# Seven products instead of eight in the last two column blocks of two output projections

## What is computed

```python
x = x + diff_attention(rms_norm(x, a_norm_g[0]), ...)       # ends in  o @ w_o      (2048 x 2048)
x = x + sq_relu_mlp(rms_norm(x, mlp_norm_g[0]), w_up[0], w_down[0])
k_nope, k_rope, v = shared_latent_kv(x, ...)
x = x + mla_attention(rms_norm(x, b_norm_g[0]), ...)        # ends in  o @ b_w_o    (2048 x 2048)
x = x + sq_relu_mlp(rms_norm(x, mlp_norm_g[1]), w_up[1], w_down[1])
return rms_norm(x, final_norm_g)
```

## Time and profile before

| | us |
|---|---|
| median of 3 runs | 1980.34 (1980.28 to 1980.65) |
| the profiled execution, its own time | 1980.67 |
| its span | 1977.9 |
| PE busy (matmul) | 1968.6 |
| DVE busy | 1649.0 |
| ACT busy | 1221.1 |

### The profile page before, as it was taken

How to read it: one execution, slowest core, us unless ns; L and a number is a source line. 1 busy time by engine, 2 the same in 40 slices (tenths; PEclk the granted TensorE clock), 3 DMA queues, 4 the chain that set the end, 5 groups by cost and what they waited for, 6 DMA issues and landing times.

```text
span 1977.9 us, 24520 instructions
## 1 busy us (share of the span) xinstructions
PE 1968.6 (100%) x9080; PEld 1641.7 (83%) x9080; DVE 1649.0 (83%) x2015; ACT 1221.1 (62%) x1563; POOL 34.4 (2%) x45
## 2 busy tenths in 40 slices
PE   9999999999999999999999999999999999999998
PEld 7888888888888888888888998888888888888887
DVE  7789996678988998898886787667998898898886
ACT  6555555557667566656656665556566666666663
POOL 0000000000000000000000000000000000000000
PEclk9999999999999999999999999999999999999999
DMA  8655546766787587677666554676587678658663
GB/s 306 214 171 188 175 167 204 225 199 216 224 243 232 189 243 234 218 231 225 224 213 213 146 152 143 229 222 223 194 231 234 224 228 241 207 205 256 216 233 118
DMA packets 269405, 418.23 MB, mean 211 GB/s; under 512 B 18800, under 2 KB 88816, under 8 KB 269296
## 3 DMA queue, kind: packets, MB, share of 16 engines
q1 hardware_dynamic: 254096, 396.87, 61.1%
q0 software_dynamic: 3456, 12.58, 3.4%
q10 hardware_dynamic: 11744, 7.34, 1.3%
HBM read 379.00 MB, written 2.10 MB: 193 GB/s over the span
## 4 chain that ended last, share of the span: by engine, by line
PE 97%; issue 2%; DVE 0%; ACT 0%; POOL 0%; POOLq 0%; DVEq 0%; ACTq 0%
PE acc L617 23%; PE acc L619 23%; PE acc L618 23%; PE side L852 3%; PE side L853 3%; PE side L851 3%; PE acc L851 2%; PE acc L853 2%; PE acc L852 2%; PE acc L637 2%; PE acc L638 2%; PE acc L639 2%; PE acc L966 1%; PE acc L967 1%; PE acc L968 1%
## 5 line engine op out<-in xcount | busy, mean ns | idle before, releaser
L1745 DVE TENSOR_TENSOR wlo<-raw,whi 128x1024 fp32r<-128x1024 f32 (+2 forms) x564 | 669.5, 1204 | 141.5 <-ACT whi L1113 139.9
L1113 ACT ACTIVATE whi<-raw 128x1024 fp32r<-128x1024 f32 (+2 forms) x564 | 579.2, 1046 | 331.1 <-PE acc L619 264.3
L617 PE MATMUL acc<-whi,opA 128*128 128x512 f32 (+2 forms) x1072 | 414.7, 387 | 0.0
L619 PE MATMUL acc<-whi,opA 128*128 128x512 f32 (+2 forms) x1072 | 413.9, 386 | 0.0
L618 PE MATMUL acc<-wlo,opA 128*128 128x512 f32 (+2 forms) x1072 | 413.8, 386 | 0.0
L617 PE MATMUL acc<-whi,opB 128*128 128x512 f32 x976 | 381.1, 390 | 0.0
L619 PE MATMUL acc<-whi,opB 128*128 128x512 f32 x976 | 380.0, 389 | 0.0
L618 PE MATMUL acc<-wlo,opB 128*128 128x512 f32 x976 | 379.8, 389 | 0.0
L619 PEld LDWEIGHTS acc<-whi,opA 128*128 128x128 f32 x1072 | 201.3, 188 | 40.2
L617 PEld LDWEIGHTS acc<-whi,opA 128*128 128x128 f32 x1072 | 201.3, 188 | 40.0
L618 PEld LDWEIGHTS acc<-wlo,opA 128*128 128x128 f32 x1072 | 201.3, 188 | 40.0
(11 more groups left out here) (382 smaller groups left out, 2733.9 us busy)
## 6 DMA issues: line engine op xcount, KB each, us to landing
raw<-in_w_up SPq DMA_DIRECT2D x128, 1024.0 KB, 5.9
raw<-in_w_down SPq DMA_DIRECT2D x128, 1024.0 KB, 5.1
raw<-in_a_w_qkv SPq DMA_DIRECT2D x44, 1024.0 KB, 5.1
prob<-o_sb SPq DMA_DIRECT2D x136, 128.0 KB, 2.6
raw<-in_a_w_o SPq DMA_DIRECT2D x16, 1024.0 KB, 5.1
raw<-in_b_w_o SPq DMA_DIRECT2D x16, 1024.0 KB, 5.1
raw<-in_w_ukv SPq DMA_DIRECT2D x32, 256.0 KB, 4.2
xs<-junk POOLq DMA_DIRECT2D x12, 512.0 KB, 5.3
```

The source lines that it names most:

```text
L617: mm(o, a_hi, w_hi, start=start, stop=False)
L619: done = mm(o, a_lo, w_hi, start=False, stop=last and c == chunks - 1)
L1113: done = fn(whi[:, place:place + ch, 0:n], raw[:, r, c0:c0 + ch, 0:n], ACT.Copy)
L1745: done = tt_(wlo[:, place:place + ch, 0:n], raw[:, r, c0:c0 + ch, 0:n], whi[:, place:place + ch, 0:n].bitcast(F32), ALU.subtract)
```

## The change

In each output projection blocks 0 and 1 stay plain, and so do row chunks 0 to 7 and 12 to 15 of blocks 2 and 3. Row chunks 8 to 11 of blocks 2 and 3 together become one group of `seven`. The functions `seven`, `shares_free`, `combine`, `form_sums`, `form_low`, `form_high`, `copy_shared`, `low` and `down_form` are moved out of `mlp` unchanged so that `out_proj` can call them, and the counts by which groups, shares and form sets are numbered take the new group in. What is new:

```diff
@@ SP @@
-            with sp.Fori(0, JB) as j:
-                whole(B_WO + j, W_O, NB * j)
+            def out_proj(b0, w, v0):
+                with sp.Fori(0, 2) as j:
+                    whole(b0 + j, w, NB * j)
+                for i, (j, r) in enumerate(((2, 0), (2, 1), (2, 2), (3, 2), (2, 3), (3, 0), (3, 1), (3, 3))):
+                    quad(b0 + 2 + i // 4, i % 4, w[:, 4 * r:4 * r + 4, NB * j:NB * j + NB], later=int(i == 6))
+                    if i in (1, 4):
+                        move_chunk(v0 + i // 4)
@@ PE @@
-                for j in range(1, JB):
-                    s = (j + 1) % 2
-                    block_tok(b0 + j, s, uses[s] + j // 2, opB)
+                block_tok(b0 + 1, 0, uses[0], opB)
+                b = b0 + 2
+                for hf in range(4):
+                    half_tok(b, hf, 1, chunks_of(opB, 2 * hf), first=hf == 0, uses=uses[1] + 1)
+                shares_free(SHARE["out", l])
+                pe.wait_ge(form_lo, FORM_SETS * l + 1)
+                seven(GROUP["out", l], b, 4, opB, 8, [forms[0][:, i] for i in range(2)], uses[0] + 1, True, SHARED)
+                for hf in range(2):
+                    half_tok(b + 1, hf, 1, chunks_of(opB, 12 + 2 * hf), last=hf == 1)
+                for hf in range(2, 8):
+                    half_tok(b + 1, hf, 0, chunks_of(opB, 2 * hf - 4 if hf < 6 else 2 * hf), first=hf == 2, last=hf == 7,
+                             uses=uses[0] + 1, starts=(False, True))
@@ ACT @@
                 x_squares(v0, 1, uses[1] + 1)
-                for j in range(1, JB):
-                    s = (j + 1) % 2
-                    body(b0 + j, {4: lambda: x_move(v0 + j - 1), 7: lambda: x_hi(v0 + j - 1, gain)})
-                    x_squares(v0 + j, s, uses[s] + j // 2 + 1)
+                body(b0 + 1, {6: lambda: form_high(forms[0][:, 0], FORM_SETS * l),
+                              7: lambda: x_hi(v0, gain)})
+                x_squares(v0 + 1, 0, uses[0] + 1)
+                b = b0 + 2
+                split(b, 3)
+                seven(GROUP["out", l], b, 4, (2, b), (3, b), {"T4": lambda: x_hi(v0 + 1, gain)})
+                for hf in range(4):
+                    split(b + 1, hf)
+                act.wait_ge(xsq, 2 * (v0 + 2))
+                copy_shared()
+                for hf in range(4, 8):
+                    split(b + 1, hf)
+                act.wait_ge(out_added, 2 * l + 2)
+                x_squares(v0 + 2, 1, uses[1] + 2)
+                split(b + 2, 0)
+                x_move(v0 + 2)
+                split(b + 2, 1)
+                split(b + 2, 2)
+                x_hi(v0 + 2, gain)
+                x_squares(v0 + 3, 0, uses[0] + 2)
@@ DVE @@
                 add_product(b0, 1, uses[1], slice(0, NB))
                 x_turn(v0, 1, 2 * (uses[1] + 1))
-                for j in range(1, JB):
-                    s = (j + 1) % 2
-                    body(b0 + j, {7: lambda: x_lo(v0 + j - 1, gain)})
-                    add_product(b0 + j, s, uses[s] + j // 2, slice(NB * j, NB * j + NB))
-                    x_turn(v0 + j, s, 2 * (uses[s] + j // 2 + 1))
+                body(b0 + 1, {4: out_form_sums, 7: lambda: x_lo(v0, gain),
+                              8: lambda: form_low(down_form(0), FORM_SETS * l)})
+                add_product(b0 + 1, 0, uses[0], slice(NB, 2 * NB))
+                x_turn(v0 + 1, 0, 2 * (uses[0] + 1))
+                b = b0 + 2
+                seven(GROUP["out", l], b, 4, (2, b), (3, b), 8 * b + 3,
+                      {"first sum": lambda: split(b, 3), "T4": lambda: x_lo(v0 + 1, gain)})
+                for hf in range(4):
+                    split(b + 1, hf)
+                combine(SHARE["out", l], down_shared)
+                split(b + 1, 4)
+                dve.wait_ge(pe_halves, 8 * b + 10)
+                add_product(None, 1, uses[1] + 1, slice(2 * NB, 3 * NB))
+                split(b + 1, 5)
+                dve.wait_ge(drained[1], 2 * (uses[1] + 2))
+                share_added()
+                split(b + 1, 6)
+                dve.wait_ge(out_added, 2 * l + 2)
+                x_turn(v0 + 2, 1, 2 * (uses[1] + 2))
+                split(b + 1, 7)
+                split(b + 2, 0)
+                split(b + 2, 1)
+                split(b + 2, 2)
+                x_lo(v0 + 2, gain)
+                add_product(b + 1, 0, uses[0] + 1, slice(3 * NB, 4 * NB))
+                x_turn(v0 + 3, 0, 2 * (uses[0] + 2))
```

More of the change, by code:

```diff
@@ new lines, in copy_shared, with seven @@
+            def copy_shared():
+                for k in range(4):
+                    fn(down_shared[k], side[k], ACT.Copy).then_inc(shared_copied, 1)
+            def seven(group, b, hf0, own, other, between):
+                (o, o_loads), (t, t_loads) = own, other
+                source = {"B11": raw[:, o, 0:2, :], "B21": raw[:, o, 2:4, :], "B22": raw[:, t, 2:4, :],
+                          "T1": w_sum, "T2": raw[:, t, 2:4, :], "T3": raw[:, t, 0:2, :], "T4": w_sum}
+                for f in FORMS:
+                    if f in SUMS:
+                        act.wait_ge(w_summed, 4 * group + SUMS[f])
+                    elif f == "B22":
+                        act.wait_ge(raw_ready[t], 16 * t_loads + 16)
+                    else:
+                        act.wait_ge(raw_ready[o], 16 * o_loads + 16)
+                    if f in IN_EXTRA:
+                        e = extra_number(group, f)
+                        if e >= 2:
+                            act.wait_ge(pe_extra, e - 1)
+                        place = 2 * (e % 2)
+                        fn(extra_hi[:, place:place + 2, :], source[f], ACT.Copy).then_inc(extra_hi_ready, 1)
+                    else:
+                        hf = hf0 + IN_RING.index(f)
+                        act.wait_ge(pe_halves, 8 * b + hf - 3)
+                        fn(whi[:, 2 * (hf % 4):2 * (hf % 4) + 2, :], source[f], ACT.Copy).then_inc(hi_ready, 1)
+                    if f in between:
+                        between[f]()
@@ new lines, in seven @@
+            def seven(group, b, hf0, own, other, lows_before, after):
+                (o, o_loads), (t, t_loads) = own, other
+                n, e = 4 * group, 3 * group
+                b11, b21 = raw[:, o, 0:2, :], raw[:, o, 2:4, :]
+                b12, b22 = raw[:, t, 0:2, :], raw[:, t, 2:4, :]
+                dve.wait_ge(raw_ready[o], 16 * o_loads + 16)
+                dve.wait_ge(raw_ready[t], 16 * t_loads + 16)
+                dve.wait_ge(lo_ready, lows_before)
+                tt_(w_sum, b11, b12, ALU.add).then_inc(w_summed, 1)
+                after["first sum"]()
+                dve.wait_ge(w_summed, n + 1)
+                tt_(b12, b12, b22, ALU.add).then_inc(w_summed, 1)
+                if "second sum" in after:
+                    after["second sum"]()
+                low("B22", group, b, hf0, b22)
+                low("T1", group, b, hf0, w_sum)
+                dve.wait_ge(w_summed, n + 2)
+                dve.wait_ge(lo_ready, 8 * b + hf0 + 1)
+                tt_(b22, w_sum, b22, ALU.add).then_inc(w_summed, 1)
+                low("B21", group, b, hf0, b21)
+                dve.wait_ge(w_summed, n + 3)
+                dve.wait_ge(extra_lo_ready, e + 1)
+                tt_(w_sum, b22, b21, ALU.add).then_inc(w_summed, 1)
+                low("B11", group, b, hf0, b11)
+                if "B11" in after:
+                    after["B11"]()
+                low("T2", group, b, hf0, b22)
+                if "T2" in after:
+                    after["T2"]()
+                low("T3", group, b, hf0, b12)
+                dve.wait_ge(w_summed, n + 4)
+                low("T4", group, b, hf0, w_sum)
+                if "T4" in after:
+                    after["T4"]()
```

271 lines of the change are left out of this document (111 added, 160 removed).

## The result

The changed kernel takes **1986.48 us** (median of 10 runs, 1984.90 to 1989.31) against 1980.43 for the kernel before (10 runs, 1979.70 to 1981.27): a ratio of 1.0032, with a 95% interval of 1.0022 to 1.0041. It is slower, by 6.05 us. I had said 1982.9, from 1977.7 to 1986.0, and most likely "no change": the range misses it by 0.5 us, and the likeliest case was the wrong one. The profiled execution is 1985.44 long, against 1980.67 before; their spans are 1983.5 and 1977.9.

What follows compares the result with a forecast made beforehand. PE was taken to bound the kernel: -2.3 us on its list and +4.9 in two waits made +2.6, so 1982.9 us against the median, range 1977.7 to 1986.0.

Steps and rivals of the forecast that it cites:

- no change: Whole kernel: within 0.2% (4.0 us) of before, on the slow side; this outcome was given 63%.
- The landings: Third and fourth chunks' moves, first issue to last landing: 8.0 to 9.6 us, taken as 8.9 for all four.
- what PE saves: PE's list in the output projections: a group's 42 matmuls replace 48 plain ones, saving 1.15 us a layer, 2.3 in both.
- the group does not starve PE: Output projection blocks with the group: DVE's work fits, so no PE wait; the rival that it starves PE had 5%.
- The half microsecond: First half behind the group, layer 0: remainder ready at 356.4, PE wants it at 357.0, so no wait counted.
- my 0.3: DVE between the second and third turn: no gap over 0.3 us expected in the changed profile.
- The two turns: DVE, layer 0: third turn ends some 57 us after block 0's addition begins (before 46.9), fourth some 71.5 (before 68.6).
- the moves again 8.9: Fourth chunk's moves behind its turn at 386.3: 8.9 us, then rounding and remainder 2.2, complete at 397.5; PE waits 2.4.
- the rival of the long landings: Third and fourth chunks' moves as long as their own before, 8.55 to 9.65 us: +4.2, 1984.5 us; chance 30%.
- break-even at 8.25 us: Third and fourth chunks' moves: two landings of 8.25 us are the break-even.
- behind each turn the change keeps their order: SP's weight loads beside ACT's moves: order unchanged behind each turn; sharing engines packet by packet speaks for late landings.
- Moving the first two chunks' moves there I cost at nothing either way: First two chunks' moves put on SP: no cost or gain, since the up projection reads them only two blocks later.

Runs made afterwards that it cites:

- experiment 4: The change, but with the first two chunks' moves issued by ACT again instead of SP: 1987.99 us, ratio 1.0037.
- experiment 5: The change, but with the third chunk's turn behind the last remainder of block 3 instead of ahead of it: 1982.45 us, ratio 1.0008.
- experiment 1: The change, but with the third and fourth chunks' moves issued by SP too, between the loads: 1978.19 us, ratio 0.9989.
- experiment 7: The change, plus 8 and 18 unused matmuls on PE ahead of the fourth and seventh half, where it waits: 1985.54 us, ratio 1.0028.
- experiment 8: The kernel before, all products plain and no group, with all four chunks' moves issued by SP: 1980.17 us, ratio 0.9997.
- experiment 6: The kernel before, without the group, with the third turn late, just ahead of the last remainder of block 3: 1982.93 us, ratio 1.0014.
- 9: The change with only the third chunk's moves put on SP, the fourth's left on ACT: 1978.33 us, ratio 0.9989.
- experiment 10: The change with only the fourth chunk's moves put on SP, the third's left on ACT: 1979.55 us, ratio 0.9996.

## Why the prediction was wrong, point by point

The way from 1982.9 to 1986.48 has three parts. The landings, mis-sized, make +1.6: 1984.5. The clock, put at nothing, makes about +1.2: taking 1.7 us off each of the six runs for every fall that its mean clock suggests (one at 0.998, two at 0.997, as in the profiled executions of experiments 4 and 5) leaves a median of 1985.3. That is an estimate, and it would have lain within my range. The 0.8 us between 1984.5 and 1985.3 stay open.

**Right: what PE saves.** 12 matmuls fewer; with the waits taken away (experiment 1) 1.8 us are left of the 2.3, and the interval of the ratio, 0.4 to 4.0 us, holds both.

**Right: the group does not starve PE.** No wait in 65 us. The half microsecond held. One gap of DVE between the turns was over my 0.3: it waited 0.40 us for ACT's copies at 360.74.

**Right: the schedule and the mechanism.** The two turns came within 0.2 us of where I had put them. PE idles in the first up block only, at the fourth and the seventh half, and the earlier wait is absorbed: in layer 0 the two together are 3.0 us, as much as the later one alone would cost a PE that came 1.15 us sooner than before.

**Wrong in size: "the moves again 8.9".** This is the term of the sum that failed first. I took the mean of eight landings of the earlier trace rows for all four, though the third and fourth chunks' own were longer. The four measured ones are 37.2 us together, not 35.6. That sum is exactly that of the rival of the long landings (9.45 + 9.65 + 9.55 + 8.55), which I gave 30%. It said 1984.5, and the runs with a full clock have 1984.90 to 1985.44. With a break-even at 8.25 us, and a slope of one for every landing, 0.4 us of choice four times over was the difference between "same" and "slower".

**Missing: the clock.** I priced a wait of PE at its length and put what follows it at nothing. The earlier trace rows show 1.00 throughout, and PE never idled there; nothing in them shows what an idle does. Six of the ten runs have a lower mean clock. One fall costs 1.7 us (experiments 4 and 5), and with the waits filled no run shows one (7). The runs at 0.999 have a median of 1985.06; by the estimate above it is the falls that take the median of all, 1986.48, past my upper end of 1986.0. The Trainium skill, "TensorE: Matmul & The Clock Gate", section "Part 1: The HAM clock gate (the "warmup" mystery)", has the two levels, 1.2 and 2.4 GHz, and that an idle PE loses the higher one. Experiment 4 agrees, with starts 0.43 us apart behind the wait instead of 0.227, and I had not weighed it.

**Right, but not used: "behind each turn the change keeps their order".** In the kernel before, too, a load goes out 1.2 us behind the first of the four moves, at all eight chunks, since the remainder that lets it go follows the turn. SP's and ACT's timelines at the third chunk of layer 0, first before, then in the change:

```profile
361.80 2.65 ACTq L1144 DMA_DIRECT2D prob<-o_sb  x4
363.04 0.37 SPq L385 DMA_DIRECT2D raw<-in_w_up  x1
```

```profile
372.52 4.36 ACTq L1161 DMA_DIRECT2D prob<-o_sb  x4
373.75 0.37 SPq L386 DMA_DIRECT2D raw<-in_w_up  x1
```

So the change did not bring the long landings; it took away the slack in which they had cost nothing (experiment 8). What I missed is that their length can be chosen: I treated it as a property of the queue, and it depends on where the next 1 MB load falls among the four moves. Experiment 5 put the load ahead of the moves and took back 4 us of the 6.

**Half right: what the queue costs.** "Moving the first two chunks' moves there I cost at nothing either way": experiment 4 is 1.5 us above the change, within its runs, and 8 shows nothing. But the two chunks that mattered are those which the change left on ACT: on SP they are worth 8.3 us. I had weighed the rule of the Trainium skill, "DMA: Bandwidth & Descriptors", section "Queues, rings and completion order", that the engines go round between the queues that have work. Landings of 2.6 to 3.6 us ahead of the loads on SP's own queue, against up to 7.8 on ACT's beside them, agree with it. But SP's queue alone does not make them short: the first chunk's moves, which the change issues on SP 0.5 us behind a load (319.88 and 320.37 in layer 0), land after 4.6 to 5.3 us, and in layer 1 of experiment 5 ACT's moves behind the load are as quick, at 5.2 us from the first move to the rounding, as SP's are in experiment 1. No run issued the moves on ACT with the load held back, so queue and order are not fully told apart. The same page's section "Issuing engines are not separate DMA queues" says that another issuing engine only saves the time of the issue. Here the choice is worth more than three times what the group saves (8.3 us against 2.3), by all that the runs show through the order against the loads.

## What to carry to other kernels

When a change makes a buffer's contents late, look at every transfer behind it for what the other queue sends at that moment: here small moves that are waited for did best on the queue of the large loads, ahead of the next load, and not beside it. A wait given to a PE that never idled cost its length and, in some executions, a stretch at half the clock on top. And where a forecast hangs on a size with a slope of one and little slack, take that size from the very transfers in question, not from a mean over all of their kind.

## What the hardware showed that I had not expected

- A wait of some 2 us was followed by a fall of the granted clock in some executions and not in others. The changed kernel's profiled execution had distances of 2.34 and 2.17 us between starts and no fall, that of experiment 5 had 2.17 us and one. One of the 21 runs of the kernel before beside experiments 9 and 10 has 0.998 too (1982.77 us), though that kernel's profiled execution has no such wait. What decides it is open.
- Four issues on ACT's queue took 2.64 us at most places, but 4.36 at 372.52 in the changed kernel and 4.06 in experiment 6. SP's loads don't explain it: before, a load went out at the same distance behind the first issue and the four took 2.65, and in experiment 1 SP itself took 3.60 for them with no load in between. What holds them up is open.
- With the clock full in all runs, experiment 7 still spread over 3.5 us. The landings differ from one profiled execution to the next (the third chunk in layer 1: 9.84 us in the change, 8.4 in experiment 10, where the load goes out 1.1 us behind the first move instead of 1.2), which would do it; it was not shown. They need not be all of it: the kernel before, which has no such waits, spread from 1979.46 to 1982.71 at 0.999 beside experiments 5 to 8, and block 0's addition, ahead of all that was changed, begins at 314.75 to 317.41 in the twelve profiled executions.
- The best version is experiment 1, or 9, which is no different from it: 1.8 us, 0.11%, under the kernel before.
